# Later loads and later dot products for the modulation weights, and one PSUM bank exchanged, in a two-block transformer kernel

## The reference

```python
mod = silu(c) @ w_ada + b_ada                 # 6 vectors of 1024
sh_a, sc_a, gt_a, sh_m, sc_m, gt_m = split(mod, 6)
h = modulate(rmsnorm(x), sh_a, sc_a)          # needs sh_a, sc_a
out = token_mixer(h, w_in, ...)               # gated linear attention + pooling, @ w_out
x = x + gt_a * out                            # needs gt_a
h2 = modulate(rmsnorm(x), sh_m, sc_m)         # needs sh_m, sc_m
x = x + gt_m * hier_moe(h2, ...)              # 32 experts, top 2; needs gt_m
```

## Time and profile before

| | us |
|---|---|
| median of 3 runs (lowest, highest) | 1226.64 (1223.53, 1227.66) |
| profiled execution, its own time | 1223.53 |
| its span in the profile | 1221.6 |
| PE busy | 1138.7 (93%) |
| DVE busy | 707.2 (58%) |
| ACT busy | 496.2 (41%) |
| mean load rate over the span | 212 GB/s |

### The profile page before, as it was taken

The page is one execution under the profiler, slowest core; times in us unless marked ns, Lnnn a source line. Parts: engine busy times, 40 slices in busy tenths (PEclk is TensorE's granted clock), DMA queues, the critical chain, the costliest instruction groups (busy, mean ns, idle before and its releaser), DMA issues.

```text
span 1221.6 us, 19142 instructions
## 1 busy us (share of the span) xinstructions
PE 1138.7 (93%) x8030; PEld 968.9 (79%) x8030; DVE 707.2 (58%) x1110; ACT 496.2 (41%) x751; POOL 0.2 (0%) x4
## 2 busy tenths in 40 slices
PE   5898998899999996989999999799999999999986
PEld 3688878555555554889999887698889999999985
DVE  1879676323333326467555677867655676655666
ACT  3674123211111113544444534236874454443453
POOL 0000000000000000000000000000000000000000
PEclk9899868799999998999999979899999999999998
DMA  9945427999999864165554522322334646445320
GB/s 385 381 174 220 167 74 282 402 424 416 410 407 406 355 250 165 43 264 206 179 195 151 186 104 95 104 104 104 121 104 183 222 147 233 168 178 207 122 87 35
DMA packets 38153, 258.38 MB, mean 212 GB/s; under 512 B 4368, under 2 KB 5136, under 8 KB 7856
## 3 DMA queue, kind: packets, MB, share of 16 engines
q1 hardware_dynamic: 36720, 252.90, 53.6%
q10 hardware_dynamic: 1344, 4.21, 0.9%
HBM read 256.05 MB, written 1.05 MB: 210 GB/s over the span
## 4 chain that ended last, share of the span: by engine, by line
PE 83%; DVE 10%; ACT 4%; issue 2%; DMA 1%; DVEq 0%; ACTq 0%
PE bank L517 82%; DVE wl L1676 2%; ACT wh L1171 1%; DMA csts<-in_cst 1%; DVE rstd L1700 1%; DVE acc L1735 1%; DVE raw L1715 1%; DVE xt L1726 0%; PE bank L866 0%; DVE hl L1740 0%; DVE arena L1811 0%; ACT arena L1181 0%; DVE arena L1874 0%; DVE arena L2243 0%; ACT L1181 0%
## 5 line engine op out<-in xcount | busy, mean ns | idle before, releaser
L517 PE MATMUL bank<-hh,wh 128*128 128x256 f32 (+1 forms) x1256 | 368.1, 293 | 9.9 <-DVE hl L1740 6.1
L517 PE MATMUL bank<-hl,wh 128*128 128x256 f32 (+1 forms) x1256 | 362.7, 289 | 0.0
L517 PE MATMUL bank<-hh,wl 128*128 128x256 f32 (+1 forms) x1256 | 362.2, 288 | 0.0
L1676 DVE TENSOR_TENSOR wl<-raw,wh 128x1024 fp32r<-128x1024 f32 (+2 forms) x236 | 266.8, 1168 | 91.4 <-ACT wh L1171 90.3
L1171 ACT ACTIVATE wh<-raw 128x1024 fp32r<-128x1024 f32 (+2 forms) x236 | 226.8, 1006 | 78.2 <-PE bank L517 78.1
L517 PEld LDWEIGHTS bank<-hh,wh 128*128 128x128 f32 x1256 | 245.0, 195 | 16.8 <-issue 13.8
L517 PEld LDWEIGHTS bank<-hl,wh 128*128 128x128 f32 x1256 | 245.0, 195 | 2.2 <-issue 0.8
L517 PEld LDWEIGHTS bank<-hh,wl 128*128 128x128 f32 x1256 | 245.0, 195 | 1.2
L517 PE MATMUL bank<-yh,wh 128*128 128x256 f32 x512 | 146.9, 287 | 6.6 <-DVE yl L1696 3.7
L517 PE MATMUL bank<-yl,wh 128*128 128x256 f32 x512 | 146.6, 286 | 0.0
L517 PE MATMUL bank<-yh,wl 128*128 128x256 f32 x512 | 146.5, 286 | 0.0
(11 more groups left out here) (245 smaller groups left out, 1373.3 us busy)
## 6 DMA issues: line engine op xcount, KB each, us to landing
raw<-in_gu SPq DMA_DIRECT2D x40, 1024.0 KB, 11.0
arena<-in_gu SPq DMA_DIRECT2D x24, 1024.0 KB, 9.7
raw<-in_gd SPq DMA_DIRECT2D x22, 1024.0 KB, 8.5
raw<-in_w_adt SPq DMA_DIRECT2D x14, 1024.0 KB, 5.7
raw<-in_f1g SPq DMA_DIRECT2D x11, 1024.0 KB, 5.2
raw<-in_f2g SPq DMA_DIRECT2D x11, 1024.0 KB, 4.8
raw<-in_f2u SPq DMA_DIRECT2D x11, 1024.0 KB, 4.8
raw<-in_f2d SPq DMA_DIRECT2D x11, 1024.0 KB, 4.8
```

The source lines that it names most:

```text
L517: return pe.matmul(o, l, m, start=start, stop=stop, skip_group_check=True)
L1676: v.tensor_tensor(WL[slot_of[U]][:, 0:n], src, WH[slot_of[U]][:, 0:n].bitcast(f32), ALU.subtract).then_inc(S("wl"), 1)
```

## The change

Five edits.
- The order of chunks: `w_adt` comes later everywhere. Chunks 0 to 2 no longer stand before w1p 1, and chunks 12 to 15 stand around w_r, the last two behind it.
- The ring: the two buffers EARLY_H and EARLY_L leave the ring at chunk 8, and not at w1v 1, so five buffers serve the first stage.
- DVE's order: dots(0, 1, 2) and dots(3, 4, 5) leave their places; chunks 0 to 11 are spread over the pool block and the attention; w_op 1 is split after head_gate(0), and not before; dots(12 to 15) and the addition and copy for gt_m (`gate_mlp`) move into the expert stage, behind p = 0.
- ACT's order: head_gate(1) before the split of w_og 0.
- Banks: the second half of w1v 1 goes to bank 1, and not 2, and kt 0 to bank 2, and not 1.

```diff
-        add_all(("w_ada", 0, 1, 2, 3, 4, 5), ("w1ak", 0), ("w_ada", 6, 7), ("w1ak", 1), ("w1p", 0), ("w_adt", 0, 1, 2), ("w1p", 1),
-                ("w1q", 0), ("w1v", 0), ("w_adt", 3, 4, 5), ("w1v", 1), ("w1g", 0), ("w_adt", 6, 7, 8, 9), ("w1g", 1),
-                ("w_adt", 10, 11), ("w_op", 0), ("w_adt", 12), ("w_op", 1), ("w_adt", 13, 14, 15), ("w_og", 0, 1), ("w_r", 0))
+        def add_ada(*pairs):
+            for i in pairs:
+                n, c = ("w_ada", 2 * i) if i < 4 else ("w_adt", 2 * i - 8)
+                add(n, c)
+                add(n, c + 1)
+
+        add_ada(0, 1, 2)
+        add("w1ak", 0)
+        add_ada(3)
+        for n, i in [("ak", 1), ("p", 0), ("p", 1), ("q", 0), ("v", 0)]:
+            add("w1" + n, i)
+        add_ada(4)
+        add("w1v", 1)
+        add_ada(5)
+        add("w1g", 0)
...
+        add_ada(10)
+        add("w_r", 0)
+        add_ada(11)
@@
-            if c in (8, where["w1v", 1]):
-                for r in (POOLS,) if c == 8 else (EARLY_H, EARLY_L):
-                    first_in[r] = raw_last[r]
+            if c == 8:
+                first_in = {r: raw_last[r] for r in (POOLS, EARLY_H, EARLY_L)}
+                for r in first_in:
                     ring.remove(r)
@@
-        fixed((("poolw", 0), 7), (("poolw", 1), 1), (("v", 1, 0), 6), (("v", 1, 1), 2))
-        fixed((("kt", 0), 1), (("kt", 1), 4), (("kt", 2), 5), (("kt", 3), 0))
+        fixed((("poolw", 0), 7), (("poolw", 1), 1), (("v", 1, 0), 6), (("v", 1, 1), 1))
+        fixed((("kt", 0), 2), (("kt", 1), 4), (("kt", 2), 5), (("kt", 3), 0))
@@ scalar_program
             head_out(3)
+            head_gate(1)
             through("w_og", 0)
-            head_gate(1)
@@ vector_program
             through("w1p", 0)
-            dots(0, 1, 2)
@@
             decay_sums(1)
+            decay_apply(0)
             through("w1v", 0)
-            dots(3, 4, 5)
-            decay_apply(0)
             decay_sums(2)
@@
             through("w1v", 1)
             decay_apply(3)
+            dots(0, 1)
             given_back(v, first_in[EARLY_L])
             for gq in range(2):
...
+            dots(2, 3)
             through("w1g", 0)
-            dots(6, 7, 8, 9)
@@
             states(1)
             scores(2)
+            dots(7, 8)
             through("w_op", 0)
-            dots(12)
             states(3)
             scores(3)
+            dots(9)
+            head_gate(0)
             through("w_op", 1)
-            dots(13)
-            head_gate(0)
-            dots(14, 15)
+            dots(10, 11)
+            head_gate(1)
             through("w_og", 0)
-            head_gate(1)
             through("w_og", 1)
-            mod_rest(16, 48)
+            mod_rest(16, 40)
@@ grouped
+                    if p == 0:
+                        dots(12, 13, 14, 15)
+                        gate_mlp()
```

More of the change, by code:

```diff
@@ L248, in add @@
             chunks.append((a[i], a.shape[2], name not in ("w_ada", "w_adt", "w_r", "gu", "gd")))
[L250 to L253, removed]
-        add_all(("w_ada", 0, 1, 2, 3, 4, 5), ("w1ak", 0), ("w_ada", 6, 7), ("w1ak", 1), ("w1p", 0), ("w_adt", 0, 1, 2), ("w1p", 1),
-                ("w1q", 0), ("w1v", 0), ("w_adt", 3, 4, 5), ("w1v", 1), ("w1g", 0), ("w_adt", 6, 7, 8, 9), ("w1g", 1),
-                ("w_adt", 10, 11), ("w_op", 0), ("w_adt", 12), ("w_op", 1), ("w_adt", 13, 14, 15), ("w_og", 0, 1), ("w_r", 0))
+        def add_ada(*pairs):
[12 more added lines that the diff above has]
+        add("w1g", 0)
+        add_ada(6)
+        add("w1g", 1)
+        add_ada(7, 8)
+        add("w_op", 0)
+        add_ada(9)
+        add("w_op", 1)
+        add("w_og", 0)
+        add("w_og", 1)
+        add_ada(10)
+        add("w_r", 0)
+        add_ada(11)
         MERGE = [("w2gb", 0), ("w2gb", 1), ("wba", 0), ("wbb", 0), ("w2gb", 2), ("wba", 1), ("wbb", 1), ("w2gb", 3),
@@ L299, in program @@
         EXTRA_W, EXTRA_A, BETWEEN, EARLY_H, EARLY_L, POOLS = range(NR, NR + 6), range(NR + 6, NR + 11), NR + 11, NR + 12, NR + 13, NR - 1
-        raw_of, raw_no, raw_last, follows, loads, first_in = [], [], [-1] * len(RAW), [], {}, {}
+        raw_of, raw_no, raw_last, follows, loads = [], [], [-1] * len(RAW), [], {}
         ring = collections.deque([POOLS, EARLY_H, EARLY_L, 0, 1, 2, 3, BETWEEN])
         for c in range(len(chunks)):
-            if c in (8, where["w1v", 1]):
-                for r in (POOLS,) if c == 8 else (EARLY_H, EARLY_L):
-                    first_in[r] = raw_last[r]
+            if c == 8:
+                first_in = {r: raw_last[r] for r in (POOLS, EARLY_H, EARLY_L)}
+                for r in first_in:
                     ring.remove(r)
@@ L1901, in vector_program @@
             scores(0)
+            dots(4)
             through("w1g", 1)
@@ L1904, in vector_program @@
             scores(1)
-            dots(10, 11)
+            dots(5, 6)
             states(1)
             scores(2)
+            dots(7, 8)
             through("w_op", 0)
-            dots(12)
             states(3)
             scores(3)
+            dots(9)
+            head_gate(0)
             through("w_op", 1)
-            dots(13)
-            head_gate(0)
-            dots(14, 15)
+            dots(10, 11)
+            head_gate(1)
             through("w_og", 0)
-            head_gate(1)
             through("w_og", 1)
-            mod_rest(16, 48)
+            mod_rest(16, 40)
             v.tensor_tensor(GF, par("final1"), par("ffn1n"), ALU.mult)
@@ L1923, in vector_program @@
             v.tensor_copy(G2, GTA)
-            v.tensor_copy(G3, GTM)
             v.scalar_tensor_tensor(A2, MOD3[:, 32:40, 0], 1.0, par("norm2"), ALU.add, ALU.mult).then_inc(S("mod2"), 1)
@@ L2031, in vector_program, with gate_mlp @@
             v.wait_ge(*nth("g32", 2))
+            def gate_mlp():
+                mod_rest(40, 48)
+                step(v.tensor_copy(G3, GTM))
+                prev()
             def grouped():
```

## The result

The changed kernel takes 1260.06 us (median of 4 runs, 1257.35 to 1262.42), the kernel before 1226.08 us (median of 4, 1223.53 to 1227.66). The ratio is 1.0279, with a 95% interval of 1.0251 to 1.0306: 34.0 us slower, where 28.9 were forecast. The profiled execution of the changed kernel took 1262.93 us, with a span of 1260.7; against the span of before that is 39.1 us.

The account below looks back on a forecast made before the run. PE held 83% of the chain of waits and DVE 10%, so an edit costs what it makes PE wait. Front 17.5 plus expert stage 11.4 made 28.9 us on 1226.6: forecast 1255.5 us, range 1239 to 1267.

Parts of the forecast that it names:

- Loads of the first stage: First stage, five buffers for seven: loads move back but each lands before its split; 0 us, bounds 0 and +2.
- w1v 0: First stage: its DVE split stands behind decay_apply(0), so PE starts it at 90.8 in place of 87.5 us.
- w1v 1: First stage: waits for bank 1 until poolw 1 is copied out; starts 10.6 us later, PE idle 9.0 us.
- The clock: Front: one half-clock start, at w1v 1 after its wait, costs 2.0 us; bounds 0 and twice that.
- states(3): Attention: DVE does dots(7, 8) before it where it did dots(12), one chunk more; +2.3 us, bounds 0 and 2.3.
- w_og 0: End of the attention: split behind head_gate(1), so PE waits for its low part; +2.6 us, bounds 0 and 3.
- Expert stage: Four buffers held by w_adt 12 to 15 stop SP's queue; up(3) ends 11.4 us later, bounds 10.9 and 14.9.
- Rivals 1: Expert stage: the experts' stream is not late where it counts, only the front's cost is left; 1244.1 us, chance 0.12.
- 2 (the bank is no wait): Before w1v 1: copies and dots end before PE finishes poolw, front costs 6.4 us; 1244.4 us, chance 0.12.
- Rival 4: First stage: lighter DVE removes one or two PE waits, 4 us faster; 1222.6 us, chance 0.03.
- Rival 3: Front and expert stage: the clock falls more often, four losses of 2 us, +8; 1263.5 us, chance 0.14.

Follow-up runs that it names:

- filled kernel: Changed kernel plus matmuls with unread results in three PE waits (before w1v 0, w1v 1 and up(1)): 1258.67 us, ratio 1.0275.
- the kernel with dots(8) moved: Changed kernel with old banks, held buffers last in the ring, w1v 0 and w_og 0 split earlier, and dots(8) behind scores(3): 1229.57 us, ratio 1.0032.
- the move alone: Kernel before, with w_adt 12 to 15 loaded behind w_r and dots(12 to 15) and gate_mlp in the expert stage: 1238.09 us, ratio 1.0108.
- free buffers: Changed kernel, with the four buffers holding w_adt 12 to 15 put at the ring's end when expert weights begin: 1247.05 us, ratio 1.0174.
- the last kernel: Kernel before, with dots(12 to 15) in the expert stage, held buffers last, dots(4) to dots(11) later, w1g 1 loaded before w_adt 7: 1224.26 us, ratio 0.9991.
- three kernels whose w1v 1 began 4 us earlier: Changed kernel with old banks, held buffers last, w1v 0 split earlier: 1236.14 us; also w_og 0 split earlier: 1230.32; also dots(8) later: 1229.57.

## Why the prediction was right

The direction, the two big mechanisms and every named wait were right; the sum was 5 us short. By its own steps:

- **Loads of the first stage**, 0: held. From w1q to up(0) PE waited for no load.
- **w1v 0**, start +3.3: 3.53 measured. But its 96 matmuls started at clock 0.50 and took 13.1 us (93.30 to 106.36, the start of poolw) and not 11.5. The prediction named this as a bound, and counted it at 0.
- **w1v 1**, the bank: +10.6 up to its start. Measured 3.53 + 8.71 = 12.24, of which 1.5 is the slow w1v 0. The wait is 8.96 us, forecast 9.0. The single pieces (dots 4.58, pool block 3.11 us) came as worked out from the earlier trace rows. Undoing the exchange gave 10.6 us back.
- **The clock**, +2.0: mis-sized. The two slow starts are 1.5 and 1.4 us by the landmarks, 3.0 together. In the trace of the filled kernel both are gone, and the front still ended at the same time.
- **states(3)**, +2.3: 2.52 measured. It is the second chunk, as the kernel with dots(8) moved shows.
- **w_og 0**, +2.6: the wait is 2.71 us. The lag grew by 4.2 from states(3) to the expert stage (0.91 and 3.31), and the 1.5 beyond the wait have no wait of their own in the trace. The 0.91 goes with the clock: between states(3) and w_op 1 its mean was 0.65 before (24.3 us), 0.62 in the changed kernel (25.2) and 0.59 in the filled one (26.4). The other 0.6, of which 0.4 falls at an unchanged mean clock (0.67 and 0.68 from 200.9 and 223.2 on), is open.
- **Expert stage**, +11.4: mis-sized, 14.0 measured (14.4 for the move alone). The mechanism was as said: gu 5 issued at 263.10, 3.0 us behind the split of up(0)'s result, and landed as up(1) started at 268.08; from up(5) on the period was 30.87 us again. The term was mis-sized in the stream of loads. From gu 5's landing to gu 15's the prediction has 14 loads in 6.9 + 27.3 = 34.2 us; they took 304.8 - 268.1 = 36.7. Three things make up the 2.5. The first three loads were spaced by their issue, 2.3 us, closer than a load takes (2.48 each, 0.5 us in all). The stream was slower while it started anew, by stretch:

```profile
264.00:265.00 1.00, 0.00 (x0) 0.00 (x0) 1.00 (x3) 0.00 (x0) 0.00 (x0) 0.50 1.02 139
265.00:272.00 7.00, 3.92 (x10) 1.38 (x12) 5.29 (x12) 0.00 (x0) 0.00 (x0) 0.50 1.01 413
272.00:275.00 3.00, 3.00 (x12) 0.87 (x9) 0.00 (x0) 0.00 (x0) 0.00 (x0) 0.64 0.98 339
275.00:300.00 25.00, 23.20 (x130) 11.35 (x128) 4.74 (x9) 5.09 (x10) 0.00 (x0) 1.00 1.01 423
```

The last column is GB/s. It was 423 in the steady part, as the earlier trace rows have it, and 339 at 272 to 275, which is 0.6 us. The third and largest is that a load does not have the stream to itself, as the prediction counted: later loads are in flight beside it. From 263.10 to 268.08 the mean was 285 GB/s, that is 1.35 loads of 1.049 MB moved as gu 5 landed; from there to 304.81 it was 415 GB/s, 14.5 loads. So 15.9 loads had moved when the fifteenth, gu 15, landed. The half load that this is more than at gu 5 makes 1.3 us, an estimate from these two rates.

**The rivals.** Rivals 1 (the stream is not late where it counts) and 2 (the bank is no wait) are each refuted by the kernel that makes them true: with free buffers the changed kernel is 13.0 us faster, with the old bank 10.6. Rival 4, faster since DVE has less to do, fails on the same two, and the later kernels show what it was worth: 9.2 us less of DVE in front gave nothing, and the last kernel, with 1.5 us less of waiting before w1v 1, is 2.2 us ahead in its trace up to the expert stage and not in its time. Rival 3 (four losses of 2 us, 1263.5, above the highest run) was half right. Three bursts ran at half clock behind the named waits: w1v 0 and w1v 1 lost 1.5 and 1.4 us, and up(1) 3.0 (268.08 to 278.17, for 7.09 in the earlier trace rows). The last cost next to nothing: in the filled kernel up(1) starts at full clock and the stage is 240.7 us long, not 241.2, since the load of gu 15 sets the end. Behind the waits of 1.80 and 1.31 us, which the rival counted too, the clock stayed at 1.00. The Trainium skill, TensorE: Matmul & The Clock Gate, section "HAM oscillation — how this bites in real kernels", has each burst behind a DMA wait start cold; at up(1) the trace agrees, with the clock at 0.50 in 265 to 272.

## What to carry to other kernels

When work that frees a buffer is moved later, look up which transfer takes that buffer and what is queued behind it; the cost is the delay of that whole queue less what is prefetched. It is set by when the moved work ends, and not by how much work it is. Here 9.2 us of dot products cost 12.5 us or next to nothing, depending only on the order of the buffers, and the same trap cost 2.2 us of waiting again at w1g 1. A PSUM bank exchanged for one whose copy stands behind other work on DVE is the same trap: the bank alone cost 6 us, and the moved dots in front of its copy another 4 to 5.

## What the runs showed of the hardware

- A half-clock start cost 1.5 us for 96 matmuls (13.1 against 11.5), but with two such starts removed the expert stage began no earlier in the trace: the clock was lower in two later stretches. In the same way three kernels whose w1v 1 began 4 us earlier ran the stretch behind the key transposes at 0.79 and not 1.00, and lost 3 us there.
- A stream of 1 MB loads that started anew ran at 139 GB/s in its first microsecond in the changed kernel, and at 131 in the one with the move alone. A load alone landed 4.8 us after its issue, gu 15 in the full stream 26 us after it. A second dip, 339 GB/s, came at 272 to 275, while SP issued 8 loads within 4.5 us (gd 0 to gd 3 and gu 8 to 11, 269.98 to 274.4). In the kernel with free buffers, where the loads behind the wait were spread more widely, the stream stayed at 414 to 422 in stretches of 4 us from 264 to 280. The cause of the dip was not tried.
- The start of w1q, which no experiment touched, lay between 81.25 and 83.98 us in the profiled executions. Two spans can't be compared closer than that, and the lags have to be counted from such a landmark.
